# Attention scores on row tiles of TensorE, two at a time, in place of zero-filled keys

## What is computed

```python
def diff_attn_block(q, k, v, lam):                 # "c": 4 heads, 2 maps each, 32 channels a map
    s = jnp.einsum('bqhmd,bkhmd->bhmqk', q, k).astype(jnp.float32) * q.shape[-1] ** -0.5
    p = jax.nn.softmax(s, axis=-1)
    pd = p[:, :, 0] - lam * p[:, :, 1]
    return jnp.einsum('bhqk,bkhd->bqhd', pd.astype(v.dtype), v)
...
# window_attn_latent ("b"): 8 query heads of 64 channels on 2 key heads,
# latent rows see a window of the latents and all of the context, and a sink
    s_win = jnp.einsum('bnqhgd,bnkhd->bnhgqk', qb, kb).astype(jnp.float32) * scale
    s_win = jnp.where(valid[None, :, None, None], s_win, -jnp.inf)
    s_ctx = jnp.einsum('bnqhgd,bkhd->bnhgqk', qb, k_ctx).astype(jnp.float32) * scale
    p = jax.nn.softmax(jnp.concatenate([s_win, s_ctx, s_sink], axis=-1), axis=-1)
```

## Time and profile before

| | before |
|---|---|
| median of 3 runs | 1756.17 us |
| the profiled execution | 1755.87 us |
| its span in the trace | 1753.7 us |
| mean granted TensorE clock | 0.971 of 2.4 GHz |
| PE busy | 1643.3 us (94%) |
| DVE busy | 995.4 us (57%) |
| ACT busy | 808.1 us (46%) |
| POOL busy | 112.6 us (6%) |
| line 1646, scores with padded keys | 192 records, 88.2 us busy |
| line 547, the padded copies on POOL | 20, median 1556 ns |

### The profile page before, as it was taken

One profiled execution on the slowest core, in us unless ns is written; L12 is line 12 of the kernel. 1 busy time (PEld: TensorE's weight loads), 2 busy tenths in 40 slices (PEclk: granted clock), 3 DMA queues, 4 the chain that ended last, 5 costly groups with the idle time before them and its releaser, 6 DMA issues.

```text
span 1753.7 us, 29978 instructions
## 1 busy us (share of the span) xinstructions
PE 1643.3 (94%) x10760; PEld 1389.6 (79%) x10760; DVE 995.4 (57%) x1746; ACT 808.1 (46%) x1406; POOL 112.6 (6%) x150
## 2 busy tenths in 40 slices
PE   3999999999999999999989999998999999699997
PEld 1677577688888888676789989796889989489997
DVE  2533964566555433546658865654476634766654
ACT  3423563344444322425646654534555534455543
POOL 0150000000000000160000000020000010000000
PEclk8999999999999999999989999999999999889999
DMA  9555003333333533574046668452566687636653
GB/s 382 201 193 188 18 1 121 120 108 96 96 97 85 209 99 110 175 256 138 1 177 195 180 206 320 140 158 97 215 226 183 212 311 214 241 96 185 178 163 116
DMA packets 72371, 285.12 MB, mean 163 GB/s; under 512 B 8000, under 2 KB 11328, under 8 KB 60512
## 3 DMA queue, kind: packets, MB, share of 16 engines
q1 hardware_dynamic: 58528, 187.31, 34.5%
q0 software_dynamic: 13760, 96.67, 14.6%
HBM read 282.90 MB, written 1.05 MB: 162 GB/s over the span
## 4 chain that ended last, share of the span: by engine, by line
PE 84%; DVE 9%; DMA 4%; ACT 2%; issue 1%; POOL 0%; SPq 0%; DVEq 0%; ACTq 0%
PE B L1466 22%; PE B L1468 21%; PE B L1467 21%; PE B L1487 4%; PE B L1646 3%; PE B L1676 3%; DMA RAW<-in_wdn 2%; DVE NORM L1064 2%; PE B L1664 2%; DMA MW<-in_wmod 1%; DVE SM L1124 1%; PE B L1479 1%; PE B L1481 1%; PE B L1480 1%; DVE HL L1054 1%
## 5 line engine op out<-in xcount | busy, mean ns | idle before, releaser
L1466 PE MATMUL B<-HH,WHI 128*128 128x256 f32 (+1 forms) x1872 | 607.4, 324 | 36.4 <-DVE HL L1054 21.2
L1467 PE MATMUL B<-HL,WHI 128*128 128x256 f32 (+1 forms) x1872 | 594.4, 318 | 0.0
L1468 PE MATMUL B<-HH,WLO 128*128 128x256 f32 (+1 forms) x1872 | 594.2, 317 | 0.0
L969 DVE TENSOR_TENSOR WLO<-RAW,WHI 128x1024 fp32r<-128x1024 f32 (+1 forms) x376 | 415.7, 1110 | 243.9 <-ACT WHI L613 243.3
L613 ACT ACTIVATE WHI<-RAW 128x1024 fp32r<-128x1024 f32 (+1 forms) x376 | 359.0, 959 | 242.3 <-PE B L1468 205.3
L1466 PEld LDWEIGHTS B<-HH,WHI 128*128 128x128 f32 x1872 | 362.5, 194 | 94.3 <-issue 45.8
L1468 PEld LDWEIGHTS B<-HH,WLO 128*128 128x128 f32 x1872 | 363.1, 194 | 22.2
L1467 PEld LDWEIGHTS B<-HL,WHI 128*128 128x128 f32 x1872 | 363.6, 194 | 20.2
L1466 PE MATMUL B<-MIDH,WHI 128*128 128x256 f32 (+1 forms) x704 | 220.0, 313 | 7.0 <-DVE WLO L969 6.9
L1468 PE MATMUL B<-MIDH,WLO 128*128 128x256 f32 (+1 forms) x704 | 218.5, 310 | 0.0
L1467 PE MATMUL B<-MIDL,WHI 128*128 128x256 f32 (+1 forms) x704 | 218.5, 310 | 0.0
(11 more groups left out here) (178 smaller groups left out, 1656.7 us busy)
## 6 DMA issues: line engine op xcount, KB each, us to landing
RAW<-in_wup SPq DMA_DIRECT2D x176, 512.0 KB, 3.7
GWR<-in_wmod POOLq DMA_DIRECT2D x35, 1024.0 KB, 11.0
GWA<-in_wmod POOLq DMA_DIRECT2D x25, 1024.0 KB, 6.3
RAW<-in_wdn SPq DMA_DIRECT2D x64, 384.0 KB, 3.1
RAW<-in_wproj SPq DMA_DIRECT2D x44, 512.0 KB, 4.4
RAW<-in_wdn SPq DMA_DIRECT2D x64, 320.0 KB, 3.3
GWB<-in_wmod POOLq DMA_DIRECT2D x14, 1024.0 KB, 6.0
RAW<-in_wout SPq DMA_DIRECT2D x24, 512.0 KB, 4.3
```

The costliest lines, as they stand in the source:

```text
L969: v.tensor_tensor(WL[s][:, 0:kts, :], RAW[s][:, 0:kts, :], WH[s][:, 0:kts, :].bitcast(F32), ALU.subtract).then_inc(lo_done, 1)
L1466: mm(bank[:, 0:t], wh, a, start=first and k == 0, stop=False)
L1467: mm(bank[:, 0:t], wh, b, start=False, stop=False)
L1468: ins = mm(bank[:, 0:t], wl, a, start=False, stop=stop and k == kts - 1)
```

## The change

The padded copies `KP`, their semaphore `keys_ready` and `pads` are gone. The score matmul now takes as both operands only the 32 or 64 partitions of its head or map (`store[r:r + n, ...]`), so that TensorE works as row tiles of 32 or 64 rows. `scores` takes one c item (two maps, two row tiles) or two b items (heads h and h+4, the upper and lower 64 rows of one tile) and issues both score matmuls back to back; the mask matmuls of a b pair follow both. Kind s calls it with all 128 rows as before.

```diff
@@
-        KP = sb("KP", [P, 10, 512], at=w0 + 18432)
@@
-                                maps = [(3 + h % 4, h // 4)]
+                                maps = [(3 + h % 4, 0, 64 * (h // 4), 64)]
@@
-                                maps = [(7 + h // 2, 2 + 4 * (h // 2) + 2 * (h % 2) + m) for m in range(2)]
+                                maps = [(7 + h // 2, 1 + h // 2, 64 * (h % 2) + 32 * m, 32) for m in range(2)]
@@
-            def pads(l, q):
-
-                gp.wait_ge(qrope, total([9, 9, 10], l) + q + 1)
-                for j in range(2 if q == 0 else 4):
-                    m = cst("half", j) if q == 0 else cst("strip", j)
-                    k = j if q == 0 else 2 + 4 * (q - 1) + j
-                    gp.tensor_scalar(KP[:, k, :], QK[:, q, :], m, None, ALU.mult).then_inc(keys_ready, 1)
@@
-                    if rot is not None and rot < 3 and IS_L[l]:
-                        pads(l, rot)
@@
-                    pe.wait_ge(keys_ready, 10 * l + 10)
@@
-                def scores(it):
-                    a, b = it["keys"]
-                    qt = it["qt"]
-                    for m, (q, k) in enumerate(it["maps"]):
-                        u = it["u"] + m
-                        if u >= 3:
-                            pe.wait_ge(p_done, ub + u - 2)
-                        bank = SBANK[u % 3]
-                        window = it["kind"] == "b" and qt < 2
-                        ins = mm(bank[:, 0:b - a], store[:, q, P * qt:P * qt + P], keys[:, k, a:b], start=True,
-                                 stop=not window)
-                        if window:
-
-                            c = P * (1 - qt)
-                            ins = mm(bank[:, c:c + P], BFC[:, 0, :], BFC[:, 1 + qt, :], start=False, stop=True)
-                        ins.then_inc(sc_mm, 1)
+                def scores(pair):
+                    for it in pair:
+                        a, b = it["keys"]
+                        qt = it["qt"]
+                        for m, (q, k, r, n) in enumerate(it["maps"]):
+                            u = it["u"] + m
+                            if u >= 3:
+                                pe.wait_ge(p_done, ub + u - 2)
+                            ins = mm(SBANK[u % 3][:, 0:b - a], store[r:r + n, q, P * qt:P * qt + P],
+                                     store[r:r + n, k, a:b], start=True, stop=it["kind"] != "b" or qt >= 2)
+                            if it["kind"] != "b" or qt >= 2:
+                                ins.then_inc(sc_mm, 1)
+                    for it in pair:
+                        if it["kind"] == "b" and it["qt"] < 2:
+                            c = P * (1 - it["qt"])
+                            mm(SBANK[it["u"] % 3][:, c:c + P], BFC[:, 0, :], BFC[:, 1 + it["qt"], :], start=False,
+                               stop=True).then_inc(sc_mm, 1)
@@
-                    if j < len(its):
-                        scores(its[j])
+                    if j < len(its) and its[j]["kind"] != "b":
+                        scores([its[j]])
+                    elif j < len(its) and its[j]["h"] < 4:
+                        scores([its[j], its[j + 1]])
```

More of the change, by code:

```diff
@@ L256, in build @@
             sem("qrope"), sem("chain"))
-        keys_ready, vn_ready, amix, amul, a_hi, bfc = (sem("keys_ready"), sem("vn_ready"), sem("amix"), sem("amul"),
+        vn_ready, amix, amul, a_hi, bfc = (sem("vn_ready"), sem("amix"), sem("amul"),
                                                        sem("a_hi"), sem("bfc"))
@@ L344, in items @@
                         val = lambda kt, h=h: SV[:, kt, P * (h // 4):P * (h // 4) + P]
-                        out.append(dict(kind="s", h=h, qt=qt, keys=(0, 512), maps=[(2 + h, h // 4)], val=val, grp=grp,
+                        out.append(dict(kind="s", h=h, qt=qt, keys=(0, 512), maps=[(2 + h, h // 4, 0, P)], val=val, grp=grp,
                                         col=h % 4, dv=P, last=h % 4 == 3, first=h % 4 == 0))
@@ L554, in proj @@
                         unit(*PROJ_UNITS[l][i + 2])
-                    root, _, rot = lagged(l, i)
+                    root, _, _ = lagged(l, i)
                     if root is not None:
                         spread(l, root)
-                    if rot is not None and rot < 3 and IS_L[l]:
-                        pads(l, rot)
             gp.wait_ge(cst_in, 32)
@@ L1628, in attention @@
                 ub, ib, gbs = total(NUNIT, l), total(NITEM, l), total(NGROUP, l)
-                store, keys = (QK, KP) if IS_L[l] else (SQK, SQK)
+                store = QK if IS_L[l] else SQK
                 nq = total([9, 9, 10], l)
```

## The result

The changed kernel takes 1770.13 us, the median of 4 runs (1768.94 to 1771.24), against 1756.87 us: the ratio is 1.008 (95% interval 1.0068 to 1.0093), 13 us slower, where I had forecast 1741.3, with a range of 1734 to 1752 and a chance of 0.12 for any slowdown. The profiled execution took 1770.54 us with a span of 1768.4 us. The mean clock of TensorE was 0.946 (before: 0.971).

What follows compares the result with a forecast made beforehand. PE was taken as the bound overall and in b items, DVE and a bank loop in c items. Savings 8.4 + 1.6 + 0 + 1.0 + 3.9 = 14.9 us gave 1741.3 us, range 1734 to 1752.

Steps and rivals of the forecast that it cites:

- the pair of c terms: c items' scores: 1.6 us saved with 512 keys, limited by bank wait and DVE; 0 with 256 keys.
- fourth rival: Attention: half-row work and more PE idling let the clock fall for some 40 us, adding 20 us: 1761; chance 0.05.
- sign of being wrong altogether: Inside attention: a clock below 0.95, or c steps faster than 2.85 us, would show the forecast wrong.
- Two tiles overlap almost fully: Score matmul pairs on two row tiles: 1.0 to 1.24 us instead of 1.78 serial.
- first rival: Score pairs: only neighbouring records overlap, so a pair takes 1.43 us; 10.6 us saved in all, 1745.6; chance 0.16.
- b items, 8.4 + 1.0 us: b items' paired scores: 8.4 us saved on latent rows in both layers, 1.0 us on context rows.
- Second rival: b pairs: the second matmul waits for a bank, losing half the b saving; about 1747; chance 0.13.
- The copies, 3.9 us: Layer 1's projection: without padded copies the wait for `GWB` and the slow clock behind it go, saving 3.9 us.
- c step by the bank loop, 2.9 us: c items, 512 keys: second map waits for a bank freed by the exponential, so the step stays 2.9 to 3.0 us.
- Third rival (no overlap): Row tiles do not overlap at all; tile changes and open weight loads make it 4.5 us slower, 1760.7; chance 0.09.
- The sum: Whole kernel: the terms add to 14.9 us saved from the profiled 1755.87 us.

Runs made afterwards that it cites:

- e7: Changed kernel with both maps of each c item on the same 32-row tile, so they cannot overlap; 1789.83 us, ratio 1.0187.
- e9: Changed kernel with both maps of each c item on the same 64-row tile; 1790.43 us, ratio 1.0178.
- g2: best_late_pads plus, after 12 matmuls on one 32-row tile, ten c steps' PE work without waits (layer 0) or 150 transposes (layer 1); 1836.54 us.
- g3: best_late_pads plus, after 12 matmuls on one 32-row tile, 100 value matmuls (layer 0) or 24 128-row, 512-column matmuls (layer 1); 1846.72 us.
- e4: Kernel before without the padded copies: every score matmul on all 128 partitions of the plain key tile, old order; 1751.05 us, ratio 0.9969.
- e1: Changed kernel with only the b items on row tiles in pairs; c items on 128-row matmuls with 8 padded key copies per layer; 1749.67 us, ratio 0.9961.
- g kernels: Three versions of best_late_pads: before each attention, 12 matmuls on one 32-row tile to halve the clock, then a burst; 1860.35, 1836.54, 1846.72 us.
- e3: Changed kernel with five extra 128-row matmuls of 512 columns ahead of item 1's scores in each attention, filling PE's idle gap; 1770.63 us, ratio 1.0082.
- f2: best_late_pads with a burst ahead of each attention: 24 matmuls on one 32-row tile (layer 0), on one 64-row tile (layer 1); 1798.62 us.
- f1: best_late_pads with a burst ahead of each attention: 24 pairs on two 32-row tiles (layer 0), on two 64-row tiles (layer 1); 1784.97 us.
- e5: Changed kernel's pair order for b items, but every score matmul on all 128 partitions of the plain key tile, no copies; 1751.51 us, ratio 0.9977.
- best_late_pads: Changed kernel with c items on padded keys, their 8 copies spread over projection slots 8 to 15; b pairs on row tiles; 1749.31 us, ratio 0.9947.
- e6: best_late_pads with b items on 64-row tiles issued one by one; seven runs 1758.21 to 1761.70 us, five 1814.19 to 1817.49.
- f4: best_late_pads with a burst ahead of each attention: 120 value matmuls (layer 0), twelve groups of a 32-row pair and one 128-row matmul (layer 1); 1796.73 us.
- g1: best_late_pads plus, after 12 matmuls on one 32-row tile, 24 pairs on two 32-row tiles (layer 0) or 24 single 64-row matmuls (layer 1); 1860.35 us.

## Why the prediction was wrong

- **The step that failed** is the pair of c terms, a saving of "1.6 us, bounds 0 and 2.6" for 512 keys and "0, bounds -0.8 and +0.4" for 256. They measured a loss of 17.6 us (7.7 in layer 0 and 9.9 in layer 1) and one of 6.2; in layer 0 the items with 256 keys begin at 197.83 us before and at 204.53 after. I took the clock of 1.00 of the earlier trace rows as given for work of another shape. My fourth rival named this mechanism, "work on half the rows, with PE idling more", at 0.05 and 1761 us; its price was also too small, 40 us of slow work where some 65 us ran slow in layer 0 and 34 in layer 1, and it stood outside my range. The earlier trace rows had shown a clock at half after one short wait, and the first waits of attention had dropped it before too (0.66 in 175 to 180 us), from where it came back within the c items. What I missed is that with score matmuls on 32 or 64 rows it does not come back there, with PE just as busy (e7, e9, and g2 without any wait), while 128-row matmuls lift it (g3). Filling up the rows in `KP` was doing that; the zeros themselves do not matter, as e4, which keeps the clock up on plain keys, and g3 show. In e1, with 128-row c items, the clock came back from such a dip within 5 us. The prediction's own sign of being wrong altogether, a clock below 0.95 inside attention, is what came.
- **How it fails, as the g kernels show it**: a wait early in the c items (3.81 us in the changed kernel, 1.60 with the gap filled) takes the clock down, and nothing in a c step on 32-row tiles lifts it; the b pairs, two 64-row tiles side by side beside transposes, do. That waits together with row tiles caused the fall in e3 is inferred from its timeline. The one matmul behind its 1.60 us wait ran alone on a 32-row tile, and that alone lowers a full clock (f2), so what part the wait has in it stays open; no run had the c items on tiles without their waits from full clock on.
- **Two tiles overlap almost fully**: right. 1.06 us for the pair against 1.0 to 1.24. The first rival (neighbours only, 1.43) falls. "TensorE: Matmul & The Clock Gate", Part 3, of the Trainium skill, taken with strict order of all records, would have given it; the trace does not agree. In f1 the first records of both tiles start at 170.09 and 170.10 us and both second ones at 170.63.
- **b items, 8.4 + 1.0 us**: right in mechanism, a little large. e1 measures 8.1, with the c items 1.0 us shorter in layer 0 and 1.2 longer in layer 1. In layer 1, latent rows only, it is 4.4 where half of 8.4 was forecast; layer 0 has 3.7 where the other half and the 1.0 were. Second rival: e5 shows that the order alone costs nothing. With tiles a plain context pair takes 2.13 us against 2.18; what is missing in layer 0, 1.5 us, is no more than the same b items differ by between two profiles (64.43 us in e1, 65.92 in best_late_pads), so its cause stays open.
- **The copies, 3.9 us**: right; 4.1 us in the changed kernel, 4.3 and 4.4 in e5 and e4.
- **c step by the bank loop, 2.9 us**: not tested, since no run had a c item on tiles at full clock without filler.
- **Third rival (no overlap)**: falls for pairs. For a lone row tile e6 shows a price of 0.20 us an item, close to the 0.2 that I had put on a pair that does not overlap.
- **The sum**: the spans came out 29.6 us from my 14.9 us saved. 25.4 of it lie in the c items and 3.6 in the b items, of which 2.4 are the slow first pairs of layer 0 (66.86 us against 64.43 in e1).

## What to carry to other kernels

Before taking rows out of matmuls, look at what lifts the clock after the waits near them: zero-padded or otherwise wasteful full-height matmuls may be the only work there that does. Row tiles pay where PE is the bound and where the pairs and the work beside them lift the clock (here the b pairs: 3.84 us instead of 4.50 for a plain pair on latent rows). In this kernel they did not pay in the c items, which begin with waits. A clock of 1.00 in the profile before belongs to the matmuls that ran there, so price a change of their shape at both levels.

## What the runs showed of the hardware

- What keeps a full clock need not lift it (one execution of each burst). Two 32-row tiles, one 64-row tile and 64-column value matmuls kept 1.00 for 20 to 26 us (f1, f2, f4) and did not lift 0.50 in 40 to 42 us (g1, g3), with PE busy throughout.
- One 32-row tile alone brought 1.00 down to 0.50 about 4 us after its start (f2), 3 us in g3, with PE busy.
- Plain fp32 transposes lifted the clock (from 0.50 to 1.00 within 4 us, g2), and 128-row matmuls of 512 columns within 6 us (g3).
- Two fp32 matmuls of 512 columns on two row tiles took 1.06 us from start to the next 128-row matmul, where one takes 0.89.
